# Spare buffers, moved casts and moved multiplies in a one-core hybrid block (recurrence, attention, gated MLP)

## The reference

```python
u = rms_norm(h, norm_mix_g)                      # 512 tokens x 2048 features, float32
rx, rgate, q, k, v, iq, ik, iw, gate_a, gate_b = split(u @ w_in)
xc = causal_depthwise_conv(rx, conv_w, conv_b)   # 4 taps
r, i = sigmoid(block_diag(xc, w_r, b_r)), sigmoid(block_diag(xc, w_i, b_i))
log_a = -8 * r * softplus(-lam);  a = exp(log_a)
y = scan(a, sqrt(-expm1(2 * log_a)) * i * xc)    # along the tokens
ya = y * gelu(rgate)                             # 1024 channels
yb = top-k sparse attention(q, k, v, iq, ik, iw) # 8 heads of 128
mixed = sigmoid(gate_a) * (ya @ w_branch_rnn) + sigmoid(gate_b) * (yb @ w_branch_attn)
h = h + mixed @ w_out
h = h + square(relu(rms_norm(h) @ w_mlp_up)) @ w_mlp_down
out = rms_norm(h, norm_final_g)
```

## Time and profile before

| | before |
|---|---|
| median of 3 runs | 2579.46 us (2577.68 to 2581.14) |
| profiled execution | 2582.11 us, span 2580.3 us |
| TensorE busy | 2518.6 us, 98% |
| VectorE busy | 1953.6 us, 76% |
| ScalarE busy | 1278.7 us, 50% |
| GpSimd busy | 578.4 us, 22% |
| mean granted TensorE clock | 0.991 |

### The profile page before, as it was taken

One profiled execution on the slowest core, in us unless ns is written; L12 is line 12 of the kernel. 1 busy time (PEld: TensorE's weight loads), 2 busy tenths in 40 slices (PEclk: granted clock), 3 DMA queues, 4 the chain that ended last, 5 costly groups with the idle time before them and its releaser, 6 DMA issues.

```text
span 2580.3 us, 35447 instructions
## 1 busy us (share of the span) xinstructions
PE 2518.6 (98%) x13123; PEld 2172.4 (84%) x13123; DVE 1953.6 (76%) x2054; ACT 1278.7 (50%) x1622; POOL 578.4 (22%) x458
## 2 busy tenths in 40 slices
PE   9989978999989999999999999999999999999998
PEld 8878867888878788878889999999998888888886
DVE  5758754456368997963388888888888999999997
ACT  6332355334344445432365666566665555554555
POOL 2550221001200220010001122111211254343443
PEclk9999999999989999999999999999999999999999
DMA  5472322322556565464436666566658776445652
GB/s 195 149 254 86 100 70 70 94 74 74 206 218 240 206 232 190 176 163 133 149 110 191 204 208 191 183 205 202 202 183 328 278 235 251 171 174 211 243 212 82
DMA packets 257151, 460.91 MB, mean 179 GB/s; under 512 B 10368, under 2 KB 150240, under 8 KB 243744
## 3 DMA queue, kind: packets, MB, share of 16 engines
q1 hardware_dynamic: 243920, 414.87, 46.4%
q0 software_dynamic: 12880, 44.57, 5.9%
q10 hardware_dynamic: 256, 0.18, 0.0%
HBM read 366.13 MB, written 93.32 MB: 178 GB/s over the span
## 4 chain that ended last, share of the span: by engine, by line
PE 85%; DVE 6%; issue 3%; ACT 3%; DMA 2%; POOL 1%; ACTq 0%; POOLq 0%; DVEq 0%
PE stream L2288 8%; PE stream L2289 7%; PE stream L2290 7%; PE stream L2706 4%; PE stream L2708 4%; PE stream L2707 4%; PE aux L2708 4%; PE aux L2707 4%; PE aux L2706 4%; PE aux L2678 3%; PE stream L2678 3%; PE aux L2685 2%; PE aux L2683 2%; PE aux L2684 2%; PE stream L2683 2%
## 5 line engine op out<-in xcount | busy, mean ns | idle before, releaser
L1558 DVE TENSOR_TENSOR wlo<-raw,whi 128x2048 fp32r<-128x2048 f32 x72 | 171.6, 2384 | 199.3 <-ACT whi L942 199.3
L903 POOL TENSOR_TENSOR hh<-hh,dn_tmp 128x512 f32<-128x512 f32 x112 | 219.0, 1977 | 328.6 <-ACT dn_tmp L1452 328.6
L2288 PE MATMUL stream<-uhi,whi 128*128 128x512 f32 (+1 forms) x640 | 244.8, 383 | 9.4 <-DVE wlo L1558 3.7
L1491 ACT CAST dhi<-d 128x1024 fp32r<-128x1024 f32 x160 | 167.6, 1053 | 162.4 <-PE aux L2708 97.4
L2289 PE MATMUL stream<-ulo,whi 128*128 128x512 f32 (+1 forms) x640 | 243.6, 381 | 0.0
L2290 PE MATMUL stream<-uhi,wlo 128*128 128x512 f32 (+1 forms) x640 | 243.4, 380 | 0.0
L942 ACT CAST whi<-raw 128x2048 fp32r<-128x2048 f32 x72 | 137.4, 1908 | 213.3 <-PE stream L2290 213.3
L2216 DVE TENSOR_TENSOR dlo<-d,dhi 128x1024 fp32r<-128x1024 f32 x160 | 228.2, 1444 | 11.5 <-ACT dhi L1491 11.4
L2706 PE MATMUL stream<-dhi,dsum 128*128 128x512 f32 x448 | 174.4, 389 | 1.2 <-DVE hh L2141 1.2
L2707 PE MATMUL stream<-dlo,dsum 128*128 128x512 f32 x448 | 174.3, 389 | 0.0
L2708 PE MATMUL stream<-dhi,dsum 128*128 128x512 f32 x448 | 174.3, 389 | 0.0
(11 more groups left out here) (411 smaller groups left out, 7504.0 us busy)
## 6 DMA issues: line engine op xcount, KB each, us to landing
d<-in_w_mlp_down SPq DMA_DIRECT2D x64, 1024.0 KB, 7.5
dsum<-sums_d SPq DMA_DIRECT2D x56, 1024.0 KB, 10.7
raw<-in_w_in SPq DMA_DIRECT2D x48, 1024.0 KB, 5.1
g<-in_w_in SPq DMA_DIRECT2D x32, 1024.0 KB, 7.2
up_b<-in_w_mlp_up SPq DMA_DIRECT2D x32, 1024.0 KB, 11.4
up_a<-in_w_mlp_up SPq DMA_DIRECT2D x32, 1024.0 KB, 9.8
gsum<-usum_d SPq DMA_DIRECT2D x28, 1024.0 KB, 9.9
sums_d<-hlo SPq DMA_DIRECT2D x32, 896.0 KB, 4.2
```

The lines of the kernel that those rows point to most:

```text
L903: pool.tensor_tensor(v, v, dn_tmp[r][:], ALU.add).then_inc(s.dn_p, 1)
L1491: nc.scalar.copy(dhi[m % 7][:], parts[j]).then_inc(s.half_hi, 1)
L1558: V.tensor_tensor(wlo[slot][:, 0:width], raw[slot][:, 0:width], whi[slot][:, 0:width].bitcast(F32), ALU.subtract).then_inc(s.lo_ready, 1)
L2288: T.matmul(dst, ah, bh, start=first and k == 0, stop=False)
```

## The change

Token sums: `us` becomes two buffers, and GpSimd forms the sums of k+1 before it issues the transfers of k. Recurrence: `xcs` gets a third buffer; `bdhi` gets a semaphore of its own and a place after the following unit's split; `lru_first`, `lru_parts`, `lru_low` and `lru_conv` move to earlier units; GpSimd makes `bdlo` of group i+1 before `lru_out(i)`; `lru_low(i)` and the `bdhi` copy now wait for the block products of group i-1. Attention sums: `y_sums_hi` and `y_sums_lo` move to earlier units. The last `rnn_out` moves behind the cast of half m = 3 of gate step 0, and TensorE begins that step with two of four banks copied out. The multiplies by the gates go from GpSimd to VectorE (`gate_times`), in steps 3, 4 and 9 ahead of the low parts of m = 8 and m = 10.

```diff
-    xcs = [at("xc0", R4 + 32, [P, 2, S], F32), at("xc1", R3 + 16, [P, 2, S], F32)]
+    xcs = [at("xc0", R4 + 32, [P, 2, S], F32), at("xc1", R3 + 16, [P, 2, S], F32), at("xc2", R3 + 24, [P, 2, S], F32)]
...
-    us = at("us", 168, [P, 4, half_s], F32)
+    us = [at("us0", 168, [P, 4, half_s], F32), at("us1", 160, [P, 4, half_s], F32)]
@@ GpSimd @@
+        def spill_u(k):
             pool.wait_ge(s.tok_lo, k + 1)
             for c, v in enumerate((ushi, uslo)):
...
         for k in range(KP):
+            if k == 1:
+                pool.wait_ge(s.rsb_t, 1)
             if k:
-                pool.wait_ge(s.tok_lo, k)
+                pool.wait_ge(s.tok_add, 5 * k)
+            if k >= 2:
+                pool.wait_ge(s.tok_lo, k - 1)
+            v = us[k % 2]
...
+            if k:
+                spill_u(k - 1)
+        spill_u(KP - 1)
...
         def lru_pool(i):
-            pool.wait_ge(s.lru_hi, 3 * i + 1)
+            pool.wait_ge(s.bd_hi, i + 1)
             pool.tensor_tensor(bdlo[:], bd[:], bdhi[:].bitcast(F32), ALU.subtract).then_inc(s.bd_lo, 1)
+            if i < 3:
+                pool.wait_ge(s.bd_lo, i + 1)
+                load_bd(i + 1)
...
         lru_pool(0)
         for i in range(4):
             if i < 3:
-                pool.wait_ge(s.bd_lo, i + 1)
-                load_bd(i + 1)
+                lru_pool(i + 1)
             lru_out(i)
-            if i < 3:
-                lru_pool(i + 1)
...
         for n in range(2):
-            for e, b in enumerate((2 * n + 1, 2 * n)):
-                pool.wait_ge(s.gate_sig, 2 * n + e + 1)
-                pool.tensor_tensor(acc_r[b][:], acc_r[b][:], acc_g[b][:], ALU.mult).then_inc(s.gate_mul, 1)
             pool.wait_ge(s.gate_mul, 2 * n + 2)
...
         for k, b in enumerate((1, 0, 3, 2)):
-            if k < 2:
-                pool.wait_ge(s.gate_sig, 4 + k + 1)
-                pool.tensor_tensor(acc_r[b][:], acc_r[b][:], acc_g[b][:], ALU.mult).then_inc(s.gate_mul, 1)
             pool.wait_ge(s.gate_mul, 4 + k + 1)
@@ ScalarE @@
+        def lru_blocks(i):
+            act.wait_ge(s.bd_in, 128 * i + 128)
+            act.wait_ge(s.lru_mm, 2 * i)
+            nc.scalar.copy(bdhi[:], bd[:]).then_inc(s.bd_hi, 1)
...
                 if v == 0:
+                    lru_first(1)
+                    lru_blocks(0)
                     lru_parts(0)
+                elif v == 1:
+                    lru_first(2)
+                    lru_parts(1)
+                elif v == 5:
+                    lru_first(3)
                 elif v % 2 == 0:
-                    lru_first(v // 2)
-                    lru_gate(v // 2 - 1)
-                    lru_mult(v // 2 - 1)
-                    lru_parts(v // 2)
-                elif v > 1:
-                    lru_hi_out(v // 2 - 1)
+                    k = v // 2
+                    if k == 3:
+                        lru_parts(3)
+                    lru_blocks(k)
+                    if k >= 2:
+                        lru_hi_out(k - 2)
+                    lru_gate(k - 1)
+                    lru_mult(k - 1)
+                    if k == 1:
+                        lru_parts(2)
...
             if p == 0:
+                lru_hi_out(2)
                 lru_gate(3)
                 lru_mult(3)
...
         v_hi(6)
+        y_sums_hi(0)
         pt_copy(6, (4, 7, 6))
...
         rnn_hi(3)
+        y_sums_hi(1)
         yb_copy(3, 1)
-        y_sums_hi(0)
         rnn_hi(4)
         rnn_out(1)
-        y_sums_hi(1)
+        y_sums_hi(2)
         rnn_hi(5)
-        y_sums_hi(2)
         rnn_hi(6)
+        y_sums_hi(3)
         rnn_out(2)
-        y_sums_hi(3)
         rnn_hi(7)
-        rnn_out(3)
...
+                if st == 0 and m == 3:
+                    rnn_out(3)
@@ VectorE @@
         def lru_low(i):
             for j in range(2):
-                dve.wait_ge(s.lru_hi, 3 * i + j + 2)
+                dve.wait_ge(s.lru_hi, 2 * i + j + 1)
+                dve.wait_ge(s.lru_mm, 2 * i)
...
         for v in range(8):
             next_lo(U_HD, 4, v // 4, v % 4)
             k = v // 2
-            if v % 2 == 0:
+            if v < 2:
+                if v:
+                    lru_low(0)
+                lru_conv(v)
+            elif v % 2 == 0:
                 if k >= 2:
                     lru_out_lo(k - 2)
-                lru_conv(k)
-                if k:
-                    lru_var(k - 1)
+                lru_low(k)
+                if k == 1:
+                    lru_conv(2)
+                lru_var(k - 1)
             else:
-                lru_low(k)
-                if k:
-                    lru_scan(k - 1)
+                lru_scan(k - 1)
+                if k == 2:
+                    lru_conv(3)
...
+        def gate_times(b, k):
+            dve.wait_ge(s.gate_sig, k)
+            V.tensor_tensor(acc_r[b][:], acc_r[b][:], acc_g[b][:], ALU.mult).then_inc(s.gate_mul, 1)
...
+                if st in (3, 4, 9) and m in (8, 10):
+                    gate_times({3: 1, 4: 3, 9: 1}[st] - (m == 10), {3: 1, 4: 3, 9: 5}[st] + (m == 10))
@@ TensorE @@
+                    if j == 1 and st == 0:
+                        pe.wait_ge(s.drained, B_WO)
...
-        pe.wait_ge(s.drained, B_WO)
+        pe.wait_ge(s.drained, B_WO - 2)
```

More of the change, by code:

```diff
@@ L789, in _ @@
                                    v[:, e:e + 2].bitcast(F32)).then_inc(s.tok_sp, 16)
+        for k in range(KP):
+            if k == 1:
[5 more added lines that the diff above has]
+            v = us[k % 2]
+            pool.tensor_tensor(ur[:], uhi[:, 2 * k:2 * k + 2].bitcast(F32), ulo[:, 2 * k:2 * k + 2].bitcast(F32),
+                               ALU.add).then_inc(s.tok_add, 1)
+            pool.wait_ge(s.tok_add, 5 * k + 1)
+            a11, a21, a12, a22 = ur[:, 0, 0:HALF], ur[:, 0, HALF:S], ur[:, 1, 0:HALF], ur[:, 1, HALF:S]
+            pool.tensor_tensor(v[:, 0], a21, a22, ALU.subtract).then_inc(s.tok_add, 1)
+            pool.tensor_tensor(v[:, 2], a11, a21, ALU.subtract).then_inc(s.tok_add, 1)
+            pool.wait_ge(s.tok_add, 5 * k + 2)
+            pool.tensor_tensor(v[:, 1], v[:, 0], a11, ALU.subtract).then_inc(s.tok_add, 1)
+            pool.wait_ge(s.tok_add, 5 * k + 4)
+            pool.tensor_tensor(v[:, 3], v[:, 1], a12, ALU.add).then_inc(s.tok_add, 1)
+            if k:
+                spill_u(k - 1)
+        spill_u(KP - 1)
         for g in range(2):
@@ L1017, in u_sums_hi @@
                 act.wait_ge(s.tok_sp, 64 * k)
-            nc.scalar.copy(ushi[:], us[:]).then_inc(s.tok_hi, 1)
+            nc.scalar.copy(ushi[:], us[k % 2][:]).then_inc(s.tok_hi, 1)
         for i in range(2):
@@ L1059, in lru_first @@
             for j in range(2):
[L1060 to L1061 removed]
+                if i >= 3:
+                    act.wait_ge(s.lru_v, lru_dve(i - 3, "lo", j))
                 c = 2 * i + j
[L1063 removed]
+                nc.scalar.activation(xcs[i % 3][:, j], rx[:, c], ACT.Identity,
                                      scale=par[:, PR_CW + 24 + c:PR_CW + 24 + c + 1],
                                      bias=par[:, PR_CB + c:PR_CB + c + 1]).then_inc(s.lru_c0, 1)
+        def lru_blocks(i):
+            act.wait_ge(s.bd_in, 128 * i + 128)
+            act.wait_ge(s.lru_mm, 2 * i)
+            nc.scalar.copy(bdhi[:], bd[:]).then_inc(s.bd_hi, 1)
         def lru_parts(i):
[L1068 to L1069 removed]
             for j in range(2):
                 act.wait_ge(s.lru_c, 6 * i + 4 + j + 1)
[L1072 removed]
+                nc.scalar.copy(yahi[:, 2 * i + j, 0:S], xcs[i % 3][:, j]).then_inc(s.lru_hi, 1)
         def lru_gate(i):
@@ L1103, in lru_hi_out @@
                 act.wait_ge(s.lru_y, 2 * i + j + 1)
-                nc.scalar.copy(yahi[:, 2 * i + j, 0:S], xcs[i % 2][:, j]).then_inc(s.lru_a, 1)
+                nc.scalar.copy(yahi[:, 2 * i + j, 0:S], xcs[i % 3][:, j]).then_inc(s.lru_a, 1)
         lru_first(0)
@@ L1645, in u_sums_lo @@
             dve.wait_ge(s.tok_hi, k + 1)
-            V.tensor_tensor(uslo[:], us[:], ushi[:].bitcast(F32), ALU.subtract).then_inc(s.tok_lo, 1)
+            V.tensor_tensor(uslo[:], us[k % 2][:], ushi[:].bitcast(F32), ALU.subtract).then_inc(s.tok_lo, 1)
         for i in range(2):
@@ L1719, in lru_low @@
             for j in range(2):
-                dve.wait_ge(s.lru_hi, 3 * i + j + 2)
-                V.tensor_tensor(xclo[:, j], xcs[i % 2][:, j], yahi[:, 2 * i + j].bitcast(F32),
+                dve.wait_ge(s.lru_hi, 2 * i + j + 1)
+                dve.wait_ge(s.lru_mm, 2 * i)
+                V.tensor_tensor(xclo[:, j], xcs[i % 3][:, j], yahi[:, 2 * i + j].bitcast(F32),
                                 ALU.subtract).then_inc(s.lru_lo, 1)
@@ L1934, in mix_rest @@
                                 ALU.subtract).then_inc(s.mix_lo, 1)
-        def gate_b_mul(b, k):
-            dve.wait_ge(s.gate_sig, 4 + k)
-            V.tensor_tensor(acc_r[b][:], acc_r[b][:], acc_g[b][:], ALU.mult).then_inc(s.gate_mul, 1)
         end = GATE_RING + 14 * (GATE_STEPS - 1)
```

32 lines of the change are left out of this document (11 added, 21 removed).

## The result

The changed kernel takes 2543.57 us (median of 4 runs, 2543.01 to 2545.63), the kernel before in the same session 2580.3 (2577.68 to 2582.85). The ratio is 0.9859, 95% interval 0.9842 to 0.9876: 1.4% faster. The forecast was 2536.6 with a range of 2529 to 2548. The sign and the range hold; the forecast's own, narrower range (2532 to 2541) does not. The gain is 36.7 us where 42.9 were forecast. The profiled execution took 2545.63, its span 2543.8, and TensorE started 0.8 to 0.9 us later than in the profile of before.

What follows compares the result with a forecast made beforehand. TensorE was taken as the bound, busy 2518.6 of 2580.3 us, so only idle and low-clock time could be won. Terms 0 + 21.3 + 14.1 + 7.5 = 42.9 us gave 2536.6, range 2529 to 2548.

Steps and rivals of the forecast that it cites:

- the forecast's own, narrower range: Whole kernel: 2532 to 2541 us, from the terms' bounds and 1 us each way for runs; chance 0.60.
- Token sums, 0: Token sums: both TensorE waits stay, since landings and softplus, not the buffer, make them late; gain 0.
- Attention sums, 14.1: Attention sums and last copy: waits at WR7 and the first gate half go, with their clock loss; 14.1 us won.
- gates, 7.5: Gates: with the multiplies on VectorE all five TensorE waits go; 7.5 us won.
- the 0.4 taken: Gates, step 9: loss at `turn_mix` from the adding transfer landing late; 0.4 us, bounds 0 and 0.7.
- Recurrence, 21.3: First block products to KQ2: three `bdlo` waits go; 21.3 of 27.7 lost us won, bounds 20 and 23.
- is late next: Recurrence's tail at KQ2: 4.6 us idle in place of 2.55, plus 1.8 for the clock; 6.4 us left.
- its sign at KQ2: TensorE's list of waits has one for `vf` at KQ2, of 4 to 5 us.
- the layout: Recurrence: new orders set out in time with fixed operation lengths; block products start without a wait, KQ2 at 420.9.
- 11.9 us passed from the start of such a split to the end of the `yahi` copy behind it: Recurrence's tail: this earlier duration, applied from KQ0's split at 384.6, ends `lru_hi_out(2)` at 396.5.
- rival B: Recurrence: one more wait of the old size with its clock, 8 to 10 us, giving 2546; chance 0.14.
- rival E: ScalarE in the recurrence: table switches cost what the skill page says, 12.4 us worse, giving 2549; chance 0.02.

Runs made afterwards that it cites:

- p_token: Kernel before with only the second token-sum buffer and the spill one step later: 2578.9 us, ratio 0.9994.
- tok_slots: Changed kernel with the last three token sums' copies and low parts three units later: 2537.43 us, ratio 0.9833 to the kernel before.
- quiet: Changed kernel with VectorE held behind each scan until GpSimd ends its multiply by the gate branch: 2539.98 us, ratio 0.9843 to the kernel before.
- dve_out: Changed kernel with the recurrence's multiply by the gate branch on VectorE instead of GpSimd: 2536.61 us, ratio 0.9830 to the kernel before.
- kq_first: Changed kernel with the three recurrence buffers placed differently and KQ1's drain ahead of group 3's scan: 2536.31 us, ratio 0.9827 to the kernel before.
- kq_dve: Changed kernel with the gate-branch multiply on VectorE and KQ1's drain ahead of group 3: 2532.37 us, ratio 0.9813 to the kernel before.
- p_rec: Kernel before with only the recurrence's part of the change: 2564.65 us, ratio 0.9940.
- sp_early: Changed kernel with the softplus one unit earlier, at unit (1, 0): 2542.08 us, ratio 0.9850 to the kernel before.
- p_att: Kernel before with only the moved attention-sum spills and last copy: 2567.94 us, ratio 0.9954.

## Why the forecast was right, and where its sum was off

- **Token sums, 0.** Right: waits of 3.69 and 3.29 stand where 3.70 and 3.17 stood, for the reason given (landings, softplus), and p_token measures 1.1 (interval -0.8 to 3.9). The working took the softplus as what ends the first wait; tok_slots shows that it keeps 2.6 of the 3.7 by itself, and the second wait and the rest of the first go with the sums' places.
- **Attention sums, 14.1, and gates, 7.5.** Right in mechanism: WR7, the first gate half and all five gate waits are as described, with 0.25 at `turn_mix` for the 0.4 taken; in step 3 VectorE's low parts and sums of weights take 1.21 to 1.23 each, where they took up to 5.61. Alone they measured 12.1 and 10.0, each within its interval of the term, and together 22.1 for 21.6.
- **Recurrence, 21.3.** The three `bdlo` waits go and the clock stays at 1.00 up to KQ1's end, as laid out. The size of what "is late next" is wrong: the prediction has "4.6 us idle in place of 2.55. ... I take 1.8", and its sign at KQ2 was a wait of 4 to 5; the wait is 11.26, the clock 2.7. The part alone won 15.4 (interval 11.9 to 18.8) where 21.3 stood with bounds of 20 and 23, by the tail's 14.0 for 6.4. The step that failed is that the layout ran GpSimd's pair of products and VectorE's next work side by side at their own lengths, in each of its three places; the last of them is in the sentence "11.9 us passed from the start of such a split to the end of the `yahi` copy behind it".

Why the rows misled: in the kernel before, GpSimd's product ran while VectorE had nothing to do (the 11.9 us of the earlier trace rows hold a pair of 3.29), and the new order puts VectorE's next low part or taps beside it. In the changed kernel the same stretch at KQ0 takes 13.8 (390.28 to 404.10), which is 1.9 of the 6.7 us that the wait is too long; the rest was there before, and the delay gathers from group to group. Start of each group's table load and of KQ2, in us from KQ1's end, read from the timelines:

| | group 1 | group 2 | group 3 | KQ2 |
|---|---|---|---|---|
| laid out in the prediction | -68.7 | -42.8 | -19.8 | +4.6 |
| changed kernel | -66.2 | -38.1 | -13.2 | +11.3 |
| quiet (no overlap, product on GpSimd) | -68.2 | -39.7 | -16.8 | +7.6 |
| dve_out (product on VectorE) | -68.9 | -41.7 | -19.9 | +3.4 |

The 6.7 us by which KQ2 is later than laid out were there at group 3: 2.5 of them at group 1, 2.2 more at group 2, 1.9 more at group 3. With the overlap taken away by a wait, 3.6 of it goes; the 3.0 that stay appear at group 2, where the taps of `lru_conv(3)` now stand behind GpSimd's pair, since the work of the two engines adds up. With the product on VectorE, 2 us shorter there, the layout comes out within 1.2 at every point. So the order, the units and the ScalarE terms were right, and what was missing is that GpSimd's pair and VectorE's work add up. The remaining 0.9 of the 7.6 is the clock, 2.7 for 1.8, which three other traces have at 2.0 to 2.1 behind the same wait (last section). The prediction had the mechanism in rival B, "GpSimd's operations and VectorE's exclude each other there", but priced it as one wait of the old size between HD3 and KQ0, with a chance of 0.14. It came as a longer tail instead, and by its amount (8 to 10 us forecast, 7.6 found) the time fell between forecast and rival. That the stated range holds is owed to B's size having been put into it: the forecast's own bounds, 2532 to 2541, would have missed by 2.6.

On the Trainium skill's rule on switches (ScalarE: Activation LUTs, What ACT_TABLE_LOAD costs): the load at 404.11 takes 1.28 us and the activation behind it starts at 405.41, 1.30 later. No drain of 1.38 beside the load is seen in this trace, and none was in the kernel before; rival E is out.

What stays open: the medians give kq_first and kq_dve 2 to 3 us less than the traces do (7.3 for 9.7, 11.2 for 14.0). The difference is inside the intervals. Some 0.7 of it is the clock behind the tail, which the profiled execution of the changed kernel, 2.1 above its median, had at 2.7 for the 2.0 to 2.1 of the three others; the rest no wait accounts for.

## What to carry to other kernels

A duration read where the neighbouring engine was idle is a lower bound once the order changes: ask for each term what will run beside it in the new order, above all for GpSimd and VectorE on SBUF. A chain that goes from ScalarE to VectorE to GpSimd and back and crosses groups carries each delay to its end, so price the end of the chain and not only its largest link. Moving the product to VectorE (7.0 us) and taking the next unit's drain out of the chain (7.3) each removed part of the tail, and only both removed it. Where two engines exclude each other and one of the two operations is urgent, holding the other back by a wait can win time (3.6 us here). Before an operation is moved into a gap, compare its length with the gap's: the softplus overran its gap by 1.3 us and delayed a transfer by 2.8.

## What the runs showed of the hardware

GpSimd and VectorE took turns by whole instructions, in both directions. VectorE's low part of 2.29 us stretched to 2.89 and 3.31 beside GpSimd's products, a pair of 3.3 by itself. The same pair of operations, GpSimd's 128x512 subtraction and VectorE's low part, shows it both ways. In quiet GpSimd began first, by 0.07 us: it took 1.29, the low part 3.36.
```profile
346.35 1.29 POOL L815 TENSOR_TENSOR bdlo<-bd,bdhi 128x512 fp32r<-128x512 f32 x1
```
```profile
346.42 3.36 DVE L1578 TENSOR_TENSOR wlo<-raw,whi 128x2048 fp32r<-128x2048 f32 x1 [2.38 <-POOL xc L824]
```
In dve_out VectorE began first (346.06, 2.29 us, shown above) and had two pairs queued behind, which end at 350.76: all five ran at their own length, and the subtraction took 5.63.
```profile
346.28 5.63 POOL L815 TENSOR_TENSOR bdlo<-bd,bdhi 128x512 fp32r<-128x512 f32 x1 [13.77 <-ACT bdhi L1067]
```
By the Trainium skill (SBUF — State Buffer, Who interferes with whom) the two engines' shared port pair goes to whichever starts first, for a whole instruction, and a VectorE operation with two SBUF inputs contends with a GpSimd operation that reads SBUF. These rows agree on the lock, 3.36 for 2.29 and 5.63 for 1.29. How it passes from a busy engine to a waiting one differs in the rows. In dve_out GpSimd waited through all five VectorE operations. In the changed kernel, at 400.10, its second product waited through one, the low part to 402.29, and then ran to 403.44, ahead of `yalo`, which VectorE had started at 402.21 and which took 1.78 for 0.68. What decides between the two is not shown.

TensorE's granted clock was not set by the length of the wait alone. Ahead of KQ2, p_token waited the 2.55 us that the kernel before waited there:
```profile
444.46 0.77 PE L2298 MATMUL stream<-uhi,whi 128*128 128x512 f32 x1 [2.55 <-DVE vf L1789]
```
The 3 us behind that wait, first in p_token, then in the kernel before (columns as above):
```profile
444.46:447.50 3.04, 3.04 (x8) 2.42 (x9) 1.85 (x4) 2.90 (x3) 0.00 (x0) 0.52 0.02 5
```
```profile
443.87:446.90 3.03, 3.03 (x13) 2.52 (x14) 1.82 (x4) 2.92 (x3) 0.00 (x0) 1.00 0.02 5
```
At 0.52 it is the low level (1.2 GHz; 0.43 us from matmul to matmul in place of 0.2267), at 1.00 the high one. The low level followed 2.80, 3.38, 7.62 and 11.26 us at this place as well. What it costs does not follow the wait: about 1.4 us behind 2.55 (p_token), 1.5 behind 2.80, 2.5 behind 3.38 (dve_out) and 7.62 (quiet), 2.7 behind 11.26, but only 2.0 to 2.1 behind 11.27 or 11.28 in p_rec, tok_slots and sp_early. Ahead of group 1's block products the kernel before and p_att waited 5.17 us each and paid 1.5 and 2.9. One trace therefore neither shows that a wait of 2.55 costs no clock, nor prices the clock closer than about 1 us; the prediction's bounds of 0 and 2.9 for it were not too wide.
